# One core, hybrid decoder step: third and fourth input chunk loaded before the last two value-weight pieces, second chunk squared between two parts of the first one's rounding

## The reference

```
def rmsnorm(x, g):
    y = xf * lax.rsqrt(jnp.mean(xf * xf, axis=-1, keepdims=True) + EPS)
    return (y * g).astype(x.dtype)

h = rmsnorm(x, norm1_g)
z = h @ w_in                       # c_q | c_kv | k_rope | u | v
c_q = z[..., :OFF_KV]; c_kv = rmsnorm(z[..., OFF_KV:OFF_KR], kv_norm_g)
k_r = rope(z[..., OFF_KR:OFF_G], pos)
zg = gelu(z[..., OFF_G:])
u = zg[..., :GMLP_WIDTH]
v = layernorm(zg[..., GMLP_WIDTH:], v_norm_g, v_norm_b)
g = spatial_gate(u, v, w_spatial, b_spatial)     # chunks of 128 tokens
...                                # attention, W_out, SwiGLU, final norm
```

## Time and profile before

| | us |
|---|---|
| median of three runs | 1387.31 |
| lowest, highest | 1382.80, 1389.89 |
| the profiled execution, its own time | 1385.34 |
| its span, first to last instruction | 1383.6 |
| PE busy | 1322.4 |
| DVE busy | 838.6 |
| ACT busy | 507.7 |
| POOL busy | 432.5 |

### The profile page before, as it was taken

How to read it: one execution, slowest core, us unless ns; L and a number is a source line. 1 busy time by engine, 2 the same in 40 slices (tenths; PEclk the granted TensorE clock), 3 DMA queues, 4 the chain that set the end, 5 groups by cost and what they waited for, 6 DMA issues and landing times.

```text
span 1383.6 us, 24004 instructions
## 1 busy us (share of the span) xinstructions
PE 1322.4 (96%) x9436; PEld 1237.0 (89%) x9436; DVE 838.6 (61%) x1284; ACT 507.7 (37%) x885; POOL 432.5 (31%) x279
## 2 busy tenths in 40 slices
PE   5999999899999899899999999999999999999997
PEld 4778998788887656899899999999999999999987
DVE  4896036666665334627975444455345568988986
ACT  3413223665665424202522222222222234444461
POOL 1362333533423112565034444444444410000000
PEclk9999999999999899999999999999999999999998
DMA  7001001000005362453122221222222279766503
GB/s 242 22 31 66 32 31 48 32 1 21 16 1 195 130 237 99 167 171 102 39 79 86 79 83 63 72 83 72 82 70 72 79 260 360 260 197 233 190 1 130
DMA packets 66971, 146.34 MB, mean 106 GB/s; under 512 B 7778, under 2 KB 15330, under 8 KB 66178
## 3 DMA queue, kind: packets, MB, share of 16 engines
q1 hardware_dynamic: 66882, 145.12, 31.1%
HBM read 122.54 MB, written 22.55 MB: 105 GB/s over the span
## 4 chain that ended last, share of the span: by engine, by line
PE 81%; DVE 8%; issue 5%; DMA 3%; ACT 2%; POOL 1%; SPq 0%; POOLq 0%; DVEq 0%; ACTq 0%
PE ps L925 24%; PE ps L926 24%; PE ps L927 24%; PE ps L1162 2%; PE ps L933 1%; DMA araw<-in_w_dn 1%; PE ps L1225 1%; DVE x L2027 1%; POOL rt L731 1%; PE ps L1270 1%; DMA x<-in_x 1%; DVE mL L2377 1%; PE ps L941 1%; PE ps L1235 1%; DVE nmx L2255 0%
## 5 line engine op out<-in xcount | busy, mean ns | idle before, releaser
L894 POOL TENSOR_TENSOR ws<-wraw,ws 128x1024 fp32r<-128x1024 f32 x50 | 125.3, 2506 | 214.9 <-ACT ws L1526 214.9
L925 PE MATMUL ps<-bHL,aHL 128*128 128x272 f32 x616 | 178.2, 289 | 4.4 <-DVE bHL L2689 4.4
L927 PE MATMUL ps<-bHL,aHL 128*128 128x272 f32 x616 | 177.3, 288 | 0.0
L926 PE MATMUL ps<-bHL,aHL 128*128 128x272 f32 x616 | 177.1, 288 | 0.0
L2532 DVE TENSOR_TENSOR bufP<-bufP,ps 128x544 f32<-128x544 f32 x66 | 47.5, 721 | 131.8 <-PE ps L927 129.5
L1526 ACT ACTIVATE ws<-wraw 128x1024 fp32r<-128x1024 f32 x55 | 58.4, 1061 | 173.0 <-PE ps L927 169.0
L925 PEld LDWEIGHTS ps<-bHL,aHL 128*128 128x128 f32 x616 | 116.0, 188 | 5.4 <-DVE bHL L2689 5.3
L926 PEld LDWEIGHTS ps<-bHL,aHL 128*128 128x128 f32 x616 | 116.0, 188 | 0.0
L927 PEld LDWEIGHTS ps<-bHL,aHL 128*128 128x128 f32 x616 | 115.9, 188 | 0.0
L2269 DVE TENSOR_TENSOR pTL<-ps,pTH 128x512 fp32r<-128x512 f32 (+1 forms) x96 | 53.2, 555 | 51.3 <-ACT pTH L1526 50.7
L917 POOL TENSOR_TENSOR rt<-ms,mhalf 128x3 f32<-128x3 f32 (+1 forms) x3 | 3.0, 997 | 252.3 <-DVE ms L2719 252.3
(11 more groups left out here) (366 smaller groups left out, 4584.4 us busy)
## 6 DMA issues: line engine op xcount, KB each, us to landing
araw<-in_w_dn SPq DMA_DIRECT2D x121, 256.0 KB, 3.4
wraw<-in_w_gu SPq DMA_DIRECT2D x44, 512.0 KB, 3.6
cp<-in_cache SPq DMA_DIRECT2D x64, 272.0 KB, 4.6
ab<-acts SPq DMA_DIRECT2D x34, 272.0 KB, 4.4
raw<-in_w_out SPq DMA_DIRECT2D x16, 512.0 KB, 4.2
acts<-bufC SPq DMA_DIRECT2D x22, 272.0 KB, 2.1
x<-in_x SPq DMA_DIRECT2D x4, 1088.0 KB, 7.2
x<-x2s SPq DMA_DIRECT2D x8, 544.0 KB, 5.9
```

Of the source, the lines that this page charges most:

```text
L894: pool.tensor_tensor(w[:, 1, :], w_source(j), w[:, 0, :], ALU.subtract).then_inc(cw_lo, 1)
L925: nc.tensor.matmul(out, wh, xh, start=start, stop=False)
L926: nc.tensor.matmul(out, wh, xl, start=False, stop=False)
L927: return nc.tensor.matmul(out, wl, xh, start=False, stop=stop)
```

## The change

On SP, the loads of input chunks 2 and 3 are issued directly behind that of chunk 1, ahead of the value pieces 2 and 3. They stood behind both pieces, chunk 3 also behind the thirteen loads of constants. On ACT, the rounding of chunk 0 is cut: tiles 0 to 4, the squares of chunk 1, tiles 5 to 7. The buffers, the waits and the work are the same as before.

```diff
             load_x(1)
+            load_x(2)
+            load_x(3)
             piece(N_V + 2, d["w_v"][2])
             piece(N_V + 3, d["w_v"][3])
-            load_x(2)
             for t, name in const_loads:
                 full = tuple(slice(None) for _ in t.shape)
                 sp_.dma_start(t[full], d[name]).then_inc(ld_const, 16)
-            load_x(3)
             piece(N_SP, d["w_sp"])
...
-            def hi1(c):
+            def hi1(c, ks=range(KD)):
                 c0, n = CH1[c]
-                for k in range(KD):
+                for k in ks:
                     act.wait_ge(n1_x, KD * c + k + 1)
                     hi(hH[:, k, c0:c0 + n], x1[:, k, c0:c0 + n]).then_inc(n1_hi, 1)
 
             squares1(0)
-            hi1(0)
+            hi1(0, range(KH + 1))
             squares1(1)
+            hi1(0, range(KH + 1, KD))
             squares1(2)
             hi1(1)
```

## The result

The changed kernel takes 1395.42 us (median of five runs, 1391.63 to 1396.40), the kernel before 1386.39 us (five runs). The ratio is 1.0061 with a 95% interval of 1.0036 to 1.0085: slower by 8.5 us (5 to 12). Measured again with eleven runs beside 34 of before, it is 1.0042 (1.0025 to 1.0059), 5.8 us. Forecast was 1388.0 and no change, in a range of 1382.5 to 1392.5; the time of the first measurement lies outside it, that of the second (1392.29) just inside.

The account below looks back on a forecast made before the run. PE was taken as the bound from 31 to 107 us, with slack before. Terms +3.2 - 2.8 + 0 + 0.3 = +0.7 us on the median 1387.31 gave 1388.0 us, no change that can be told; range 1382.5 to 1392.5.

Parts of the forecast that it names:

- Chunks 2 and 3 leave early: SP's queue: issues cost some 0.6 us each, so both loads leave by about 5.5 us, before piece 2 at 10.40.
- Piece 2 waits its turn: SP's load queue: piece 2 waits 8.0 us more behind 2816 KB, lands at 21.8, its vwL ready at 24.2.
- PE 3.2 us later at the sum of chunk 1, 2.8 given back: PE: late vwL of piece 2 costs +3.2 us; the sum of chunk 2 directly behind chunk 1's spread returns -2.8.
- The gift: PE before the sum of chunk 2: its 2.8 us wait for the squares disappears, -2.8 us.
- The low clock moves: PE: the 1.7 us lost to low clock moves from the sum of chunk 2 to that of chunk 1.
- the term of 0: PE's low clock: its 1.7 us loss only moves, net 0, with bounds of -1.7 and +1.7 us.
- Behind it: After PE's sum of chunk 2: DVE's factors stay hidden, POOL's fold ends 0.9 us later, PE waits 0.3: +0.3 us.
- Sharing: Rival on the load queue: piece 2 served in turns with chunks 2 and 3, landing near 17; 1383.3 us; chance 0.15.
- Slower: Rival on the load queue: piece 2 lands at 24.5, +5.1 us with low clock and fold, 1392; chance 0.17.
- nothing in this stretch is large enough to move the time by 5 us: Sign of being wrong: the time moving by more than 5 us, which nothing in the start stretch could give.

Follow-up runs that it names:

- own buffers: Kernel before with separate, wait-free buffers for value pieces 2 and 3, chunk 2 loaded right behind them, POOL's fold free: 1386.68 us, ratio 0.9999.

## Why the prediction was wrong

- **Chunks 2 and 3 leave early:** right in effect. But SP did not issue them in 0.6 us each: the loads of chunks 1 to 3 took 6.92 us of its queue, to 10.58. That cost nothing, as piece 2 could not go before 11.93 in that execution.
- **Piece 2 waits its turn:** right. 10.67 us from issue to landing, and 10.8 to 12.2 in the six other traces with the loads moved, where 8.0 + 3.4 = 11.4 was forecast; vwL of piece 2 was ready at 24.98, 24.0 the second time (24.2 forecast). The extra wait is thus 7.3 to 8.8 us. The 6.6 that the prediction works out from the fit in the Trainium skill's "DMA: Bandwidth & Descriptors" is too short for every trace; the page gives that fit for transfers that GpSimd issues, and these are issued by SP.
- **PE 3.2 us later at the sum of chunk 1, 2.8 given back:** right within a microsecond. PE was 3.9 late at the one, 1.5 of them from the late piece 0, and 0.7 at the end of the sum of chunk 2, where the forecast had 38.4 against 38.03. The gift was priced from one execution: PE's wait for the squares of chunk 2, 2.83 us there, was 3.38, 1.91 and 0.74 us in three others with the same loads, as chunk 2 landed 8.0 to 10.6 us after its issue. On the average of the four that is 2.2 us, so early loads bring less than the trace of before promised.
- **The low clock moves:** right for the profiled executions. But the term of 0 was read from one of them, too. With the loads moved all seven traces have the low clock at the sum of chunk 1, which takes 5.2 to 6.7 us instead of 3.7; with the loads of before only two of four have it at the sum of chunk 2 (7.12 us, against 5.43 in the others). On the average the term is nearer +0.8 than 0, an estimate from half of the 1.7 us.
- **Behind it, the step that failed:** "that is 0.9 us behind PE's sum, but the spread of chunk 2 is wanted only 4 us after it, and the factors take 2.9: hidden", and "+0.3" for POOL's fold. The order of events was forecast well: norm of chunk 1 done behind the sum, squares of chunk 3 early. But the factors and the fold were priced as if DVE and POOL worked side by side. The factors took 39.81 to 45.36, 5.6 us instead of 2.9; PE waited 2.6, and the clock fell. This term was put at +0.3 and is 4.0 to 4.4 us in the four traces. With 4.2 in its place the sum is +4.6, and some +6 with the averages of the two bullets above, an estimate from few traces; +5.8 and +8.5 were measured.

Both ends of the mechanism could be read before. The trace of before has it at another place, where PE did not wait for it; DVE and POOL near 61 us:

```profile
61.20 2.22 DVE L2085 TENSOR_TENSOR hL<-x,hH 128x320 fp32r<-128x320 f32 x1
63.34 0.53 DVE L2027 SCALAR_TENSOR_TENSOR x<-x,g,ps 128x320 f32<-128x320 f32 x1
...
60.56 2.51 POOL L719 TENSOR_TENSOR spL<-raw,spH 128x1024 fp32r<-128x1024 f32 x1
```

The same hL takes 0.48 us elsewhere in that chunk, and here it ends 0.35 us after POOL's operation does (63.42 against 63.07). The Trainium skill says it outright, in "SBUF — State Buffer", in "SBUF: two separate sides" and "Who interferes with whom": the pair of SBUF ports that DVE and GpSimd share is an exclusive lock for the whole instruction, a DVE operation with two SBUF inputs asks for it while a GpSimd operation reads SBUF, and whichever starts first blocks the other. The traces here agree: 0.56 us when DVE is first by 0.17, 3.24 when POOL is first by 0.07, 0.56 when POOL has no such operation. The other side pays as well: POOL's fold takes 3.19 us when it starts 0.17 behind the diagonal, 2.93 when it starts after its end. By the prediction's own numbers ACT's squares of chunk 3 would be done at 39.0 + 2.35 = 41.35, and DVE's diagonal would start as far behind the norm's end at 39.3 as it does behind PE's sum in before (40.38 - 38.03 = 2.35), at 41.65: squares ready 0.3 us before the diagonal, so POOL first. I had asked only when each would end.

None of the rivals had it either. Sharing fell: piece 2 landed between 20.9 and 23.4 us in all seven traces, never near 17. "Slower" put its price on a piece 2 at 24.5, which did not come; that its 1392 is the time of the second measurement is luck. The prediction also said that nothing in this stretch is large enough to move the time by 5 us. The collision alone is 4.2.

**What stays open.** The first measurement of the changed kernel lies 2.7 us above the second, within their intervals. In its profiled execution 4.4 us more of the difference arise behind 107 us (the store of v is issued at 111.78 instead of 107.53, the span is 8.7 longer). Two stretches of low clock stand there at places where before has none, 3.4 us together:

```profile
331.00:336.00 5.00, 3.72 (x19) 3.67 (x20) 3.16 (x8) 2.78 (x10) 0.40 (x1) 0.66 0.01 3
1171.00:1175.00 4.00, 4.00 (x22) 4.00 (x21) 4.00 (x6) 1.78 (x4) 0.00 (x0) 0.57 0.94 263
```

But this part does not follow the change. From the issue of that store to the last instruction it is 1276.1 us in before and 1280.5 in the changed kernel; it is 1281.3 with ACT's order cut, whose loads are those of before, and 1276.6 in the kernel in which piece 0 is waited for, whose store is the latest of all (112.92). So it scatters by some 6 us (1275.1 to 1281.3) with either order of the loads, and the 4.4 us can't be put down to the change. What sets this scatter was not looked into.

## What to carry to other kernels

A start that moves by a few tenths of a microsecond can decide which of DVE and POOL goes first, and the loser waits until the other is done, here 2.7 us for an operation of 0.56. Wherever an edit lets one engine's chain run ahead, look at what POOL then starts, and at whether a short DVE operation on the critical path starts in the same moment; a wait that orders the two is cheap (0.7 us on POOL here, for 3.0 to 3.4 us on PE). A load that may go only once a buffer is free should have its buffer, or stay ahead of the large loads in the queue; here that took the loss away, and any gain over the kernel before is too small to be told. And a wait that is to be won back should be read from several executions: the one priced here at 2.8 us was 0.7 in another.

## What the runs showed of the hardware that I had not expected

- A 128 x 384 diagonal on DVE took 0.56 us where it started first or POOL had no large operation beside it, and 3.24 to 3.26 us beside one that had started 0.06 or 0.07 us earlier, in six traces of six.
- Piece 2, issued on a queue with two input loads ahead, 2816 KB together, landed after 10.67 us, against 3.4 without them.
- The same first weight piece was ready for POOL anywhere between 7.39 and 9.49 us into the program, over fourteen traces.
- A wait of 2.6 us on PE was followed by a low clock in the four traces with a late piece 2 and the fold free, and not in the one with own buffers, though the wait was as long. In those four a low stretch had already stood near 25 to 29 us; whether that matters is open. Own buffers, behind its wait:

```profile
40.70:45.00 4.30, 4.23 (x21) 3.41 (x21) 3.21 (x8) 1.57 (x3) 0.00 (x0) 1.00 0.00 0
```
